# C's queries, keys and values in one product of 512 columns per token tile, its square sums on ScalarE

## The reference

```python
proj = xn @ w_in
(aq, ak, av, bq, bk, bv, cq, ck, cv, dcq, dckv, dkr, gate_logits) = jnp.split(proj, offsets, axis=-1)
qc = axial_rope(rms_norm(cq.reshape(b, s, C_HEADS, HEAD_DIM), c_qn), row_pos, col_pos)
kc = axial_rope(rms_norm(ck.reshape(b, s, C_KV_HEADS, HEAD_DIM), c_kn), row_pos, col_pos)
o_c = dense_block_attention(qc.reshape(...), kc, cv.reshape(...), HEAD_DIM ** -0.5)
```

## Time and profile before

| | |
|---|---|
| median of 3 runs | 1685.01 us (1684.35 to 1686.7) |
| profiled execution | 1685.22 us, span 1683.4 us |
| busy | PE 1656.7, POOL 1091.3, DVE 827.3, ACT 462.6 us |
| mean granted clock of PE | 0.996 of full speed |

### The profile page before, as it was taken

One profiled execution on the slowest core, in us unless ns is written; L12 is line 12 of the kernel. 1 busy time (PEld: TensorE's weight loads), 2 busy tenths in 40 slices (PEclk: granted clock), 3 DMA queues, 4 the chain that ended last, 5 costly groups with the idle time before them and its releaser, 6 DMA issues. The chain is left out here.

```text
span 1683.4 us, 22074 instructions
## 1 busy us (share of the span) xinstructions
PE 1656.7 (98%) x8582; PEld 1401.9 (83%) x8582; DVE 827.3 (49%) x1488; ACT 462.6 (27%) x1063; POOL 1091.3 (65%) x1211
## 2 busy tenths in 40 slices
PE   7999999999999999999999999999999999999997
PEld 6888898878898888888987888988789988888886
DVE  6654658655466444400266546676563564443002
ACT  3451513434251111100155415134343411111000
POOL 8635557553769777677685365664455897776774
PEclk9999999999999999999999999999999999999998
DMA  5213222122222222222242131222212222222222
GB/s 208 85 51 113 86 78 79 73 76 73 78 100 89 90 98 101 84 91 99 96 140 76 50 115 62 100 76 76 75 51 100 93 88 96 100 100 77 104 88 83
DMA packets 27335, 151.40 MB, mean 90 GB/s; under 512 B 3483, under 2 KB 6811, under 8 KB 13376
## 3 DMA queue, kind: packets, MB, share of 16 engines
q1 hardware_dynamic: 22928, 140.70, 23.2%
q10 hardware_dynamic: 4304, 9.30, 1.8%
HBM read 147.88 MB, written 4.70 MB: 91 GB/s over the span
## 5 line engine op out<-in xcount | busy, mean ns | idle before, releaser
L573 POOL TENSOR_SCALAR w_hi<-raw 128x512 fp32r<-128x512 f32 (+3 forms) x576 | 365.5, 643 | 567.5 <-DMA raw<-stream 567.5
L577 POOL TENSOR_TENSOR w_lo<-raw,w_hi 128x512 fp32r<-128x512 f32 (+3 forms) x576 | 706.8, 1238 | 0.0
L625 PE MATMUL work<-h_hi,w_hi 128*128 128x512 f32 (+1 forms) x576 | 218.5, 379 | 1.4 <-DVE h_lo L1471 1.1
L626 PE MATMUL work<-h_lo,w_hi 128*128 128x512 f32 (+1 forms) x576 | 217.3, 377 | 0.0
L627 PE MATMUL work<-h_hi,w_lo 128*128 128x512 f32 (+1 forms) x576 | 217.3, 377 | 0.0
L762 PE MATMUL main<-h_lo,w_hi 128*128 128x512 f32 x512 | 207.5, 405 | 0.0
L762 PE MATMUL main<-h_hi,w_hi 128*128 128x512 f32 x512 | 205.9, 402 | 0.0
L762 PE MATMUL main<-h_hi,w_lo 128*128 128x512 f32 x512 | 204.6, 400 | 0.0
L625 PE MATMUL work<-act_hi,w_hi 128*128 128x512 f32 (+1 forms) x396 | 145.0, 366 | 0.0
L626 PE MATMUL work<-act_lo,w_hi 128*128 128x512 f32 (+1 forms) x396 | 144.7, 365 | 0.0
L627 PE MATMUL work<-act_hi,w_lo 128*128 128x512 f32 (+1 forms) x396 | 144.7, 365 | 0.0
(11 more groups left out here) (367 smaller groups left out, 3239.5 us busy)
## 6 DMA issues: line engine op xcount, KB each, us to landing
raw<-stream SPq DMA_DIRECT2D x106, 1024.0 KB, 4.8
raw<-stream SPq DMA_DIRECT2D x32, 704.0 KB, 3.9
raw<-stream SPq DMA_DIRECT2D x4, 832.0 KB, 4.5
x<-x_in ACTq DMA_DIRECT2D x4, 512.0 KB, 11.9
t_line<-t_first ACTq DMA_DIRECT2D x2, 1024.0 KB
rpb<-rpb_line ACTq DMA_DIRECT2D x32, 64.0 KB, 3.0
bias_b<-t_line ACTq DMA_DIRECT2D x2, 768.0 KB, 4.6
out<-x SPq DMA_DIRECT2D x6, 256.0 KB, 2.2
```

The costliest lines, as they stand in the source:

```text
L573: pool.tensor_scalar(w_hi[:, slot, parts[q]], raw[:, slot, parts[q]], 1.0, 0.0, ALU.mult, ALU.add).then_inc(piece_hi, 1)
L577: e = pool.tensor_tensor(w_lo[:, slot, part], raw[:, slot, part], w_hi[:, slot, part].bitcast(F32), ALU.subtract)
L625: pe.matmul(dst, a_hi, b_hi, start=first, stop=False, **kw)
L626: pe.matmul(dst, a_hi, b_lo, start=False, stop=False, **kw)
```

## The change

- The pieces Cq (256 columns, full depth) and Ckv (256 columns, full depth) become C0 and C1: all 512 columns, each for half of the depth. For each of the four token tiles TensorE makes one product C0 to C3 into a whole bank, 24 matmuls of 512 columns. Both pieces are freed after the last tile (`ends`).
- GpSimd raises `piece_split` on every quarter. For tile C0 TensorE waits quarter by quarter, and so it does for the latent pieces Dlat0 and Dlat1 at the start of a layer; `wait_piece` waits for the last quarter, as before.
- ScalarE takes a tile at a time (`c_tile`): the copy of 384 columns, six squares of 64 columns with their sums (`accum_out`), and the high part of the values.
- VectorE loses squares, sums and the second root: one root serves 24 heads and tiles, one scaling all six heads; the gains stay two. The low parts of C's values come ahead of the norm.

```diff
-A=[...], B=[("Cq", 2048), ("Ckv", 2048), ("Bkv", 2048), ("Bq", 2048)], C=[])[_b]
+A=[...], B=[("C0", 2048), ("C1", 2048), ("Bkv", 2048), ("Bq", 2048)], C=[])[_b]
...
-            ends = dict(Dup="Dkv3", Aq="Aq1", Ak="Ak1", Av="Av1", Bq="Bq1", Bkv="Bv", Cq="Cq1", Ckv="Ckv1")
+            ends = dict(Dup="Dkv3", Aq="Aq1", Ak="Ak1", Av="Av1", Bq="Bq1", Bkv="Bv", C0="C3", C1="C3")
...
-                        e = pool.tensor_tensor(w_lo[:, slot, part], raw[:, slot, part], w_hi[:, slot, part].bitcast(F32), ALU.subtract)
-                e.then_inc(piece_split, 1)
+                        pool.tensor_tensor(w_lo[:, slot, part], raw[:, slot, part], w_hi[:, slot, part].bitcast(F32), ALU.subtract).then_inc(piece_split, 1)
...
             def wait_piece(l, n):
-                pe.wait_ge(piece_split, at(l, NP_, n + 1))
+                wait_quarter(l, n, QUARTERS - 1)
+
+            def wait_quarter(l, n, q):
+                pe.wait_ge(piece_split, at(l, QUARTERS * NP_, QUARTERS * n + q + 1))
...
-                        if half == 0 and k % 4 == 0:
-                            wait_piece(l, PIECE[f"Dlat{k // 4}"])
+                        if half == 0:
+                            wait_quarter(l, k // 4, k % 4)
...
-                for name in ("Cq", "Ckv"):
-                    wait_piece(l, PIECE[name])
-                    for j in range(2):
-                        by_token(l, f"{name}{j}", PIECE[name], (2 * j, 2 * j + 1), 0, 256, 256)
+                for t in range(NT):
+                    w = WORK_AT[f"C{t}"]
+                    wait_work(l, w)
+                    for k in range(KD):
+                        n, a = PIECE[f"C{k // 4}"], 512 * (k % 4)
+                        if t == 0:
+                            wait_quarter(l, n, k % 4)
+                        mm = three(bank_of(WORK[w])[:, :], h_hi[:, k, P * t:P * t + P], h_lo[:, k, P * t:P * t + P],
+                                   w_hi[:, n % SLOTS, a:a + 512], w_lo[:, n % SLOTS, a:a + 512], k == 0, k == KD - 1)
+                    mm.then_inc(work_done, 1)
...
+                def c_tile(t):
+
+                    src, factor = bank_of(f"C{t}"), r_token[:, t:t + 1]
+                    wait_work_done(l, f"C{t}")
+                    copy(l, f"C{t}", c_tm[:, t, :], src[:, 0:384], factor)
+                    for g in range(6):
+                        e = act.activation(c_sq[:, 384 * t + HD * g:384 * t + HD * g + HD], src[:, HD * g:HD * g + HD], ACT.Square,
+                                           scale=factor, accum_out=r_in[:, 6 * t + g:6 * t + g + 1])
+                    e.then_inc(c_squared, 1)
+                    value_parts(l, "C", t, src[:, 384:512].rearrange("p (c d) -> p c d", d=HD), factor)
...
-                for i in range(5):
-                    c_slice(l, i)
                 for t in range(NT):
-                    src = bank_of(f"Ckv{t // 2}")[:, 256 * (t % 2) + P:256 * (t % 2) + 2 * P]
-                    value_parts(l, "C", t, src.rearrange("p (c d) -> p c d", d=HD), r_token[:, t:t + 1])
-                c_slice(l, 5)
+                    value_parts(l, "C", t, bank_of(f"C{t}")[:, 384:512].rearrange("p (c d) -> p c d", d=HD), r_token[:, t:t + 1])
+                c_slice(l, 0)
                 feature_tile(l, "Bk", True)
                 lo(l, "Bk", kb_lo[:, :], feature[:, 0, :], kb_hi[:, :])
-                c_slice(l, 6)
+                c_slice(l, 1)
                 feature_tile(l, "Bv", True)
-                c_slice(l, 7)
+                c_slice(l, 2)
+                c_slice(l, 3)
                 c_rotation(l, 0)
```

More of the change, by code:

```diff
@@ L60 @@
     PIECES += dict(D=[("Dlat0", 4 * N_LAT), ("Dlat1", 4 * N_LAT), ("gateD0", 2048), ("Dup", 1280), ("gateD1", 2048)],
-                   A=[("Aq", 2048), ("Ak", 2048), ("Av", 2048)], B=[("Cq", 2048), ("Ckv", 2048), ("Bkv", 2048), ("Bq", 2048)], C=[])[_b]
+                   A=[("Aq", 2048), ("Ak", 2048), ("Av", 2048)], B=[("C0", 2048), ("C1", 2048), ("Bkv", 2048), ("Bq", 2048)], C=[])[_b]
     PIECES += [(f"gate{_b}{j}", 2048) for j in dict(D=(2, 3), A=(1, 2, 3)).get(_b, range(4))]
@@ L100 @@
     WORK += dict(D=["Dlat2", "Dlat3", "Dlat0"] + [f"Dq{t}" for t in range(NT)] + [f"Dkv{t}" for t in range(NT)],
-                 A=["Aq0", "Aq1", "Ak0", "Ak1", "Av0", "Av1"], B=["Cq0", "Cq1", "Ckv0", "Ckv1", "Bk", "Bv", "Bq0", "Bq1"], C=[])[_b]
+                 A=["Aq0", "Aq1", "Ak0", "Ak1", "Av0", "Av1"], B=[f"C{t}" for t in range(NT)] + ["Bk", "Bv", "Bq0", "Bq1"], C=[])[_b]
     for _j in range(2):
@@ L160 @@
 N_SPLIT = len(SPLIT)
-COPY = [f"Dq{t}" for t in range(NT)] + [f"Dk{t}" for t in range(NT)] + ["Cq0", "Cq1", "Ckv0", "Ckv1"]
+COPY = [f"Dq{t}" for t in range(NT)] + [f"Dk{t}" for t in range(NT)] + [f"C{t}" for t in range(NT)]
 COPY_AT = {n: i for i, n in enumerate(COPY)}
@@ L443, in program @@
         c_ready = sem("c_ready")
+        c_squared = sem("c_squared")
         crossed = sem("crossed")
@@ L667, in wait_work @@
                     pe.wait_ge(feature_done, at(l, len(FEATURE), FEATURE.index(n) + 1))
-                elif n[:3] == "Ckv":
-                    wait_split(l, ("V", "C", 2 * int(n[3]) + 1))
+                elif n[0] == "C":
+                    wait_split(l, ("V", "C", int(n[1])))
                 elif n[:4] == "Dlat":
@@ L1167, in _, with copy @@
             copies = iter(COPY * L)
-            def copy(l, name, dst, src):
+            def copy(l, name, dst, src, scale=1.0):
                 assert next(copies) == name
-                act.activation(dst, src, ACT.Copy).then_inc(copied, 1)
+                act.activation(dst, src, ACT.Copy, scale=scale).then_inc(copied, 1)
             def keep(l, name, m):
@@ L1382, in feature_high @@
                     hi(l, name, dst, feature[:, n % 4, :], scale)
[L1384 to L1389, removed]
-                        value_parts(l, "C", t, src.rearrange("p (c d) -> p c d", d=HD), r_token[:, t:t + 1])
+                for t in range(NT):
+                    c_tile(t)
                 feature_high("Bk", kb_hi[:, :], 1.0)
@@ L1609, in value_parts @@
             def value_parts(l, b, t, src, scale=None):
-                last = t if b == "D" else t | 1
+                last = t if b in "DC" else t | 1
                 lo(l, ("V", b, t), value_place(1, b, t), src, value_place(0, b, t), scale, after=("V", b, last))
@@ L1615, in c_heads @@
                 return x, x.rearrange("p t (g d) -> p t g d", d=HD)
[L1617 to L1624, removed]
             def c_root(l, n):
@@ L1677, in c_slice @@
                 if i == 0:
-                    dve.wait_ge(copied, at(l, N_COPY, COPY_AT["Cq1"] + 1))
-                    c_squares(l, 0, 4)
+                    dve.wait_ge(c_squared, at(l, NT, NT))
+                    c_root(l, 6)
                 elif i == 1:
-                    c_sums(l, 4)
+                    c_scale(l, 0, 6)
                 elif i == 2:
-                    c_root(l, 16 // NT)
+                    c_gain(l, 0, 4, "cq")
                 elif i == 3:
[L1685 to L1695, removed]
                     c_gain(l, 4, 2, "ck")
@@ L1999, in weight_stream @@
                 p = piece(w_in[l][a:a + 4 * P, W_IN_AT["Dlat"]:W_IN_AT["gates"]])
+            elif name in ("C0", "C1"):
+                rows = w_in[l][4 * P * int(name[1]):4 * P * (int(name[1]) + 1)]
+                p = piece(np.concatenate([order(rows[:, W_IN_AT["Cq"]:W_IN_AT["Ckv"]].T).T, rows[:, W_IN_AT["Ckv"]:W_IN_AT["Dlat"]]], axis=1))
             elif name.startswith("gate"):
@@ L2015, in weight_stream @@
                 w = w_in[l][:, W_IN_AT[name]:W_IN_AT[name] + size // KD]
-                p = piece(order(w.T).T if name in ("Bq", "Cq") else w)
+                p = piece(order(w.T).T if name == "Bq" else w)
             assert p.shape == (P, size), (name, p.shape)
```

## The result

The changed kernel takes 1697.79 us (1696.52 to 1698.47, four runs) against 1684.88 us in the same session: a ratio of 1.0075, with a 95% interval of 1.0062 to 1.0088. It is slower, as forecast, by 12.9 us where 11.2 were worked out. Its profiled execution took 1697.16 us, span 1695.3.

A forecast was written before the change was run, and what follows sets the result against it. TensorE, busy 98% of the span, was taken as the bound. Per layer -1.22 (product) + 4.9 (wait) + 1.9 (clock) = +5.6 us, +11.2 for two layers on 1685.0: forecast 1696 us, range 1687.5 to 1702.5.

The forecast's parts named there:

- The product: C on TensorE: 96 matmuls of 512 columns replace 192 of 256, a gain of 1.22 us a layer.
- Release and landing: Bq's load, freed only after C3, leaves at 255.12; GpSimd's split begins 4.93 us later, at 260.05.
- The split: GpSimd's split of Bq: 7.40 us undisturbed, plus 3.37 us from VectorE's instructions, ending at 270.8.
- The wait: TensorE before Bq0 waits for Bq's last low part, 4.9 us a layer; 1.6 if the split is undisturbed.
- The clock: TensorE's clock drops after the wait at Bq0, costing 1.9 us a layer, with 1.4 and 2.5 as ends.
- the likeliest case: Wait at Bq0 of 4.0 to 5.4 us with clock loss 1.4 to 2.5: 1693.4 to 1698.4 us, chance 0.57.
- The edits at nothing: ScalarE's squares, VectorE's dropped work, GpSimd's increments and the quarter waits on latent pieces were costed at 0.
- What VectorE and GpSimd do to each other: During Bq's split, each VectorE instruction waits for GpSimd's running one, then delays the next; 3.37 us together.
- The rival that the load is hidden: Bq whole by 265.83, before TensorE reaches Bq0, leaving only the gain: -2.4 us, 1682.6 us; chance 0.04.

The follow-up runs named there:

- e11: e4 plus B's features before C's root, keys' gain and rotation spread out, three rotation parts moved behind the second head pair's maxima; 1681.66 us, ratio 0.998.
- e6: Changed kernel with the old C pieces, products and release; new squares, single root and quarter waits kept; 1685.19 us, ratio 0.9999 to the kernel before.
- e2: Changed kernel with VectorE's scaling and gains held back until piece Bq is split; 1689.94 us, ratio 1.0026 to the kernel before.
- e4: Changed kernel with C2 and C3 done by depth halves, so the first piece is freed earlier; 1696.15 us, ratio 1.0065 to the kernel before.
- e1: Changed kernel with Bq0 waiting for Bq quarter by quarter instead of for the whole piece; 1687.22 us, ratio 1.0009 to the kernel before.
- e8: Changed kernel with only VectorE's order changed, B's features ahead of C's root, no depth halves; 1703.95 us, ratio 1.0113 to the kernel before.
- e10: Kernel before with one change, piece Cq freed after Ckv1 instead of Cq1, so Bq loads late; 1695.84 us, ratio 1.006.

## Why the prediction was right, and where it was off

- **The product.** Forecast -1.22 us a layer; C takes 21.76 us instead of 23.03, -1.27, or 13.2 ns for each matmul that is dropped. Right, and e11 shows no wait that takes it back.
- **Release and landing.** Forecast: load away at 255.12, split begun at 260.05. Measured 255.14 and 259.98, 4.84 us from issue to split. In layer 1 it was 5.38 us (1092.17 to 1097.55), and the forecast had reckoned with 4.93 in both. Whether the second load did that is not shown: loads issued alone took from 4.8 to 5.9 us (the longest in e6), those issued in a pair 4.8 to 5.6.
- **The split.** Forecast 7.40 + 3.37 = 10.77 us; measured 10.72 and, in layer 1, 10.94. The parts agree too: in layer 0 Bk's low part cost the split 0.44 us (forecast 0.45), the scaling 1.49 (1.45), the two gains 1.39 (1.47). e2 takes scaling and gains out of it, and 2.9 us go.
- **The wait.** Forecast 4.9 us in each layer; TensorE stood idle for 4.78 and 5.52 us. In layer 1 the split began 5.57 us after C's end (1097.55 against Bk's start at 1091.98) instead of 5.03.
- **The clock.** Forecast 1.9 us, with 2.5 as its upper end. Measured 1.73 and 8.07 - 5.45 = 2.62. In layer 1 this term left its bounds, and so did the wait (5.52, with 5.4 as the upper end of the likeliest case); both together make layer 1 cost 7.0 us where 5.6 were forecast (layer 0: 5.44). The upper end of 2.5 came from the slow steps at the launch, and no run shows that these were the clock's: the granted clock of 12.7 to 18.4 is given as 1.00 there.
- **The edits at nothing.** Right. At the start of layer 1 the first two half products lie 14.46 us apart (845.32 to 859.78) where they lay 14.40 apart, so the quarter waits give nothing there; and e6, which keeps the squares, the one root and the quarter waits, stands at 0.9999. A square of 64 columns took 0.29 us, less than the 0.41 that the prediction took from one of 128.
- **What VectorE and GpSimd do to each other.** The prediction has a VectorE instruction wait for GpSimd's and then hold up the next one. That fits the wide instructions. The short steps of the root in e4 only waited: the splits beside them kept their 7.40 us.
- **The rival that the load is hidden.** Priced at -2.4 us as soon as Bq is whole in time. That price left something out, though the result did not hang on it. In e4 Bq is whole 4 us ahead of need and the kernel is 11 us slower than before: an earlier split met the root, whose ten short steps the prediction had counted at 2.76 us, and stretched it from 2.6 to 8.8 us. The gain comes out only in e11, with a new order for VectorE besides.

Left open: why the clock cost 1.73 us behind a wait of 4.78 and 2.62 behind one of 5.52, and why Bq's load took 0.5 us longer in layer 1; neither was tried.

## What to carry to other kernels

Where every tile of a loop needs all pieces of a weight, none of them is freed before the last tile. In a ring of three slots this delays the loads that follow, and here the saving in matmuls (1.3 us a layer) is small beside what the late piece cost (6.7 to 8.3 us a layer). Where GpSimd prepares weights, place VectorE's work on SBUF operands by GpSimd's free stretches and not only by what VectorE itself has room for: between e4 and e11 this turned +0.65% into -0.2% with the same arithmetic. A wait that is removed is worth its length only if the next-late operand is in time, so read the next two of them before pricing it.

## What the hardware showed that was not expected

- VectorE's short steps suffer most from GpSimd, for their length: a step on 24 columns takes 0.18 us alone, and 0.54 to 1.24 us while a split runs (e4), about one GpSimd instruction for each. `feature`, whose first operand lies in PSUM, keeps its time: 0.67 to 0.69 us in every run, beside a split or not.
- The length of one wait does not settle TensorE's clock. It stayed at 1.00 behind waits of 1.56 (e1), 1.87 (e2) and 2.08 us (e8, layer 0), and fell behind 2.26 (e8, layer 1: 0.69 from 1111.5 to 1117), 2.58, 3.27, 4.49, 4.78 and 5.52 us to steps of 0.43 us instead of 0.227. But nearly the same waits in one execution went both ways: in e10 it fell in layer 0 behind 1.47 and 0.26 us close together (1.00 from 280 to 283, 0.66 from 283 to 288) and stayed at 1.00 in layer 1 behind 1.49 and 0.26 us (1121 to 1130). It fell also in e11 behind 1.62 us near the launch (0.50 from 36.6 to 39.0). Nor is its cost fixed: the low stretch lasted some 3.2 us behind the wait of 4.78 and 5.3 behind that of 5.52.
- Matmuls whose results are not used paid: with 24 of them in the wait the changed kernel was 8.6 us slower than the kernel before instead of 12.9.
